# One transfer for the gate and up weights of a pair of experts, by halves of the contraction

## The reference, cut to what matters

```python
for e in range(N_EXPERTS):                       # 32
    gu = xt @ w_gate_up[e]                       # (n, 1024) @ (1024, 512)
    h = jax.nn.silu(gu[:, :D_EXPERT]) * gu[:, D_EXPERT:]   # D_EXPERT = 256
    y = y + gate[:, e:e + 1] * (h @ w_down[e])   # (n, 256) @ (256, 1024)
```

## Time and profile before

| | us |
|---|---|
| median of 3 runs | 611.1 (610.58 to 611.39) |
| the profiled execution, its own time | 611.46 |
| span of that execution in the trace | 609.8 |
| TensorE busy (share of the span) | 528.2 (87%) |
| VectorE busy | 363.7 (60%) |

### The profile page before, as it was taken

The page is one execution under the profiler, slowest core; times in us unless marked ns, Lnnn a source line. Parts: engine busy times, 40 slices in busy tenths (PEclk is TensorE's granted clock), DMA queues, the critical chain, the costliest instruction groups (busy, mean ns, idle before and its releaser), DMA issues.

```text
span 609.8 us, 8917 instructions
## 1 busy us (share of the span) xinstructions
PE 528.2 (87%) x3276; PEld 288.7 (47%) x3276; DVE 363.7 (60%) x718; ACT 187.9 (31%) x351; POOL 135.1 (22%) x156
## 2 busy tenths in 40 slices
PE   5999999999969988899999989989998667768772
PEld 4887888884335543345545843333332122222210
DVE  1641028388963466654247857577877676665686
ACT  1100075204143553114121232245444333332340
POOL 1001046140013761000000200333333221222231
PEclk9999999999979997999999989999999999999997
DMA  8940007670333923100787699999999999999951
GB/s 309 396 161 5 0 1 281 210 311 0 146 133 118 419 94 135 52 2 35 298 355 278 240 397 413 417 344 405 415 416 413 416 421 416 416 414 419 411 218 49
DMA packets 34010, 158.21 MB, mean 259 GB/s; under 512 B 12680, under 2 KB 12680, under 8 KB 20016
## 3 DMA queue, kind: packets, MB, share of 16 engines
q1 hardware_dynamic: 20592, 127.72, 52.3%
q0 software_dynamic: 10752, 29.59, 13.0%
q10 hardware_dynamic: 2624, 0.34, 0.4%
HBM read 160.38 MB, written 21.23 MB: 298 GB/s over the span
## 4 chain that ended last, share of the span: by engine, by line
PE 62%; DMA 21%; DVE 8%; ACT 5%; issue 3%; SPq 0%; POOL 0%; DVEq 0%; ACTq 0%; POOLq 0%
PE ps L488 22%; DMA arena_o<-in_w_gu 19%; PE ps L940 11%; PE ps L726 8%; PE ps L963 5%; PE ps L567 2%; PE ps L613 2%; PE ps L629 2%; DVE arena_s L1436 2%; ACT arena_s L1208 2%; PE ps L925 1%; PE ps L533 1%; DMA x_rows<-arena_s 1%; PE ps L650 1%; PE ps L789 1%
## 5 line engine op out<-in xcount | busy, mean ns | idle before, releaser
L940 PE MATMUL ps<-arena_w,arena_s 128*64 128x512 f32 x368 | 109.2, 605 | 24.6 <-DMA arena_w<-in_w_gu 11.5
L488 PE MATMUL ps<-arena_w 128*128 128x260 f32 (+1 forms) x448 | 100.4, 387 | 6.3 <-DMA arena_w<-in_w_in 6.3
L488 PEld LDWEIGHTS ps<-arena_w 128*128 128x128 f32 (+1 forms) x448 | 84.3, 189 | 21.9 <-DMA arena_w<-in_w_in 6.3
L940 PEld LDWEIGHTS ps<-arena_w,arena_s 128*64 128x64 f32 x368 | 33.3, 139 | 97.5 <-issue 67.7
L963 PE MATMUL ps<-arena_w,cs 128*64 128x512 f32 x184 | 56.5, 619 | 20.8 <-ACT cs L1224 20.8
L726 PE MATMUL ps<-arena_o,arena_s 128*128 128x512 f32 x128 | 59.6, 612 | 1.6 <-DVE arena_s L1560 1.6
L940 PE MATMUL ps<-arena_o,arena_s 128*64 128x512 f32 x112 | 50.2, 596 | 0.0
L1436 DVE STREAM_TRANSPOSE arena_s<-arena_w 128x1024 f32<-128x1024 f32 x36 | 41.9, 1216 | 10.7 <-PE ps L567 10.7
L2110 POOL DMA_INDIRECT first_rows<-arena_s,known x15 | 17.8, 1189 | 112.3 <-ACT arena_s L1231 103.6
L1869 DVE TENSOR_TENSOR arena_s<-arena_s,ps 128x256 f32<-128x256 f32 x16 | 6.7, 421 | 58.4 <-ACT arena_s L1220 55.2
L963 PEld LDWEIGHTS ps<-arena_w,cs 128*64 128x64 f32 x184 | 16.2, 140 | 51.1 <-issue 30.4
(11 more groups left out here) (340 smaller groups left out, 885.5 us busy)
## 6 DMA issues: line engine op xcount, KB each, us to landing
arena_w<-in_w_gu SPq DMA_DIRECT2D x46, 1024.0 KB
arena_w<-in_w_dn SPq DMA_DIRECT2D x23, 1024.0 KB
arena_o<-in_w_gu SPq DMA_DIRECT2D x14, 1024.0 KB
arena_o<-in_w_dn SPq DMA_DIRECT2D x7, 1024.0 KB
arena_w<-in_w_in SPq DMA_DIRECT2D x13, 512.0 KB, 15.1
arena_o<-in_w_out SPq DMA_DIRECT2D x1, 4096.0 KB, 13.6
arena_s<-in_w_gu SPq DMA_DIRECT2D x4, 1024.0 KB, 7.5
arena_w<-in_xT SPq DMA_DIRECT2D x4, 520.0 KB, 6.5
```

The costliest lines, as they stand in the source:

```text
L488: last = mm(ps[rows, b + n, 0:HALF], lhs(k), rhs(k)[:, n * HALF:(n + 1) * HALF], start=(k == 0), stop=(k == ks - 1))
L940: last = mm(ps[64 * e:64 * e + 64, 2 + q, :], xgT[:, k, CAP * e:CAP * (e + 1)], gu_w[2 * slots + e][:, k, :], start=(k == 0), stop=(k == K ...
```

## The change

The six slots stay. A slot's 16 KB of gate and up weights now hold one half of the contraction for both experts of a pair, and the table `GU_SLOT` says which slot has which half. A half of a pair is one transfer of 128 partitions with 16 KB each, 2 MB; the weights lie in memory in that order, so each is one contiguous stretch. Down weights stay as they were, one transfer of 1 MB for each expert, in the slot of that expert. The waits of SyncE stand where they stood; TensorE waits for 16 in place of 32 for a half. In the first loads, slot 2 gets the first half of the second pair (before: both halves of its first expert), slot 5 the first half of the third, slot 3 and slot 4 the second halves.

```diff
+GU_SLOT = [[0, 1], [2, 3], [5, 4]]
...
-        gu_w = [s[:, 0:KD * 2 * DE].rearrange("p (k n) -> p k n", k=KD) for s in slot]
+        gu_w = [s.rearrange("p (e k n) -> p e k n", e=2, k=KD // 2) for s in gu_flat]
...
-            def gate_up(j, e, half):
-                cols = slice(half * KD * DE, (half + 1) * KD * DE)
-                sp.dma_start(gu_flat[j][:, cols], w_gu[e].rearrange("o p n -> p (o n)")[:, cols]).then_inc(gu_landed[half][j // 2], 16)
+            def gate_up(q, half, pr):
+                sp.dma_start(gu_flat[GU_SLOT[q][half]], w_gu[half, pr].rearrange("o p n -> p (o n)")).then_inc(gu_landed[half][q], 16)
...
             for half in range(2):
-                for j in (0, 1):
-                    gate_up(j, slice(j, j + 1), half)
+                gate_up(0, half, slice(0, 1))
             for j in (0, 1):
                 down(j, slice(j, j + 1))
-            for half in range(2):
-                gate_up(2, slice(2, 3), half)
+            gate_up(1, 0, slice(1, 2))
             down(2, slice(2, 3))
             store_x1(1)
             store_x1(2)
             sp.wait_ge(dec_mixed, 1)
-            for half in range(2):
-                gate_up(5, slice(5, 6), half)
+            gate_up(2, 0, slice(2, 3))
             down(5, slice(5, 6))
             store_x1(3)
             sp.wait_ge(o_done, 16)
-            for half in range(2):
-                gate_up(3, slice(3, 4), half)
+            gate_up(1, 1, slice(1, 2))
             down(3, slice(3, 4))
...
-            def refill(q, e, used):
+            def refill(q, pr, used):
                 for half, done in enumerate((gu_half, gu_ps)):
                     sp.wait_ge(done, used)
-                    for n in range(2):
-                        gate_up(2 * q + n, slice(e + n, e + n + 1) if isinstance(e, int) else bass.ds(e + n, 1), half)
+                    gate_up(q, half, slice(pr, pr + 1) if isinstance(pr, int) else bass.ds(pr, 1))
                 sp.wait_ge(dn_ps, used)
...
                     for e in range(2):
                         last = mm(ps[64 * e:64 * e + 64, 2 + q, :], xgT[:, k, CAP * e:CAP * (e + 1)],
-                                  gu_w[2 * slots + e][:, k, :], start=(k == 0), stop=(k == KD - 1))
+                                  gu_w[GU_SLOT[slots][k // (KD // 2)]][:, e, k % (KD // 2), :], start=(k == 0), stop=(k == KD - 1))
...
-        "w_gu": i["w_gate_up"][pairs].reshape(NE, KD, P, 2 * DE).transpose(0, 2, 1, 3).reshape(NE, P, -1),
+        "w_gu": i["w_gate_up"][pairs].reshape(NE // 2, 2, 2, KD // 2, P, 2 * DE).transpose(2, 0, 4, 1, 3, 5).reshape(2, NE // 2, P, -1),
```

More of the change, by code:

```diff
@@ L252, in hymba_step @@
             [arena_s[:, S_SLOT + W_SLOT * n:S_SLOT + W_SLOT * (n + 1)] for n in range(2)]
-        gu_w = [s[:, 0:KD * 2 * DE].rearrange("p (k n) -> p k n", k=KD) for s in slot]
-        dn_w = [s[:, KD * 2 * DE:W_SLOT].rearrange("p (k n) -> p k n", k=2) for s in slot]
         gu_flat, dn_flat = [s[:, 0:KD * 2 * DE] for s in slot], [s[:, KD * 2 * DE:W_SLOT] for s in slot]
+        gu_w = [s.rearrange("p (e k n) -> p e k n", e=2, k=KD // 2) for s in gu_flat]
+        dn_w = [s.rearrange("p (k n) -> p k n", k=2) for s in dn_flat]
         xg = [part(arena_s, s, D) for s in S_XG]
@@ L437, in _ @@
             landed(sp, gathered[0])
-            for half in range(2):
-                gate_up(4, slice(4, 5), half)
+            gate_up(2, 1, slice(2, 3))
             down(4, slice(4, 5))
@@ L442, in _ @@
             sp.dma_start(lng2, lns[2:4].partition_broadcast(P)).then_inc(ln1_landed, 16)
-            def refill(q, e, used):
+            def refill(q, pr, used):
                 for half, done in enumerate((gu_half, gu_ps)):
                     sp.wait_ge(done, used)
-                    for n in range(2):
-                        gate_up(2 * q + n, slice(e + n, e + n + 1) if isinstance(e, int) else bass.ds(e + n, 1), half)
+                    gate_up(q, half, slice(pr, pr + 1) if isinstance(pr, int) else bass.ds(pr, 1))
                 sp.wait_ge(dn_ps, used)
                 for n in range(2):
-                    down(2 * q + n, slice(e + n, e + n + 1) if isinstance(e, int) else bass.ds(e + n, 1))
-            refill(0, 6, 1)
-            refill(1, 8, 2)
+                    down(2 * q + n, slice(2 * pr + n, 2 * pr + n + 1) if isinstance(pr, int) else bass.ds(pr * 2 + n, 1))
+            refill(0, 3, 1)
+            refill(1, 4, 2)
             sp.wait_ge(routed, 1)
@@ L457, in _ @@
             with sp.Fori(0, n_rounds * (NE // 4) - 3) as it:
-                refill(0, (it * 4 + 10) % NE, it * 2 + 4)
-                refill(1, (it * 4 + 12) % NE, it * 2 + 5)
-            refill(0, NE - 2, past + (NPAIR - 2))
+                refill(0, (it * 2 + 5) % NPAIR, it * 2 + 4)
+                refill(1, (it * 2 + 6) % NPAIR, it * 2 + 5)
+            refill(0, NPAIR - 1, past + (NPAIR - 2))
             landed(sp, outs_stored, 6)
@@ L931, in products @@
                 q, slots = n % 2, n if n < HEAD else (n - HEAD) % 2
-                landed_count = 32 if n < HEAD else nth(it, n - HEAD, 2, 32, 64) if not isinstance(it, tuple) else \
-                    it[0] * 16 + ((n - HEAD) // 2 * 32 + 64)
+                halves_landed = 16 if n < HEAD else nth(it, n - HEAD, 2, 16, 32)
+                downs_landed = 32 if n < HEAD else nth(it, n - HEAD, 2, 32, 64)
                 pe.wait_ge(xt_sb, nth(it, n, add=1))
@@ L937, in products @@
                     if k % (KD // 2) == 0:
-                        pe.wait_ge(gu_landed[k // (KD // 2)][slots], landed_count)
+                        pe.wait_ge(gu_landed[k // (KD // 2)][slots], halves_landed)
                     for e in range(2):
                         last = mm(ps[64 * e:64 * e + 64, 2 + q, :], xgT[:, k, CAP * e:CAP * (e + 1)],
-                                  gu_w[2 * slots + e][:, k, :], start=(k == 0), stop=(k == KD - 1))
+                                  gu_w[GU_SLOT[slots][k // (KD // 2)]][:, e, k % (KD // 2), :], start=(k == 0), stop=(k == KD - 1))
                     if k == KD // 2 - 1:
@@ L947, in products, with experts @@
                     turn_tokens(it, n + 1)
-                return slots, landed_count
-            def experts(it, n, slots, landed_count):
+                return slots, downs_landed
+            def experts(it, n, slots, downs_landed):
                 pe.wait_ge(h_ready, nth(it, n, add=1))
@@ L956, in experts @@
                 pe.wait_ge(ht_sb, nth(it, n, add=1))
-                pe.wait_ge(dn_landed[slots], landed_count)
+                pe.wait_ge(dn_landed[slots], downs_landed)
                 if n > 0:
```

## The result

The changed kernel takes 617.25 us (median of 4 runs, 615.59 to 618.85) against 610.84 of the kernel before in the same runs: a ratio of 1.0105, with an interval of 1.0089 to 1.0121. The forecast was 609.7 with a range of 607.8 to 612.8. In the profiled execution the span is 616.2 us, 6.4 us above the 609.8 of before.

A forecast was written before the change was run, and what follows sets the result against it. Weight loads on saturated DMA until 570.38 us, then a fixed tail, were taken as the bound. Packets 1.37 plus the store 0.05 save 1.4 us: 611.1 median to 609.7, range 607.8 to 612.8.

The forecast's parts named there:

- What bounds the kernel, and the tail behind 570.38: Gate and up weight loads saturate DMA from 399.72 to the landing at 570.38 us; behind it a fixed 39.4 us tail.
- Packets: Weight queue, 399.72 to 570.38: 16 KB rows stay one packet, 9.5 ns saved each, 1.37 us over 18 transfers.
- Tokens: Token transfers beside the weight queue, 400 to 570 us: 6.72 MB beside 63.25 MB, bytes and packets unchanged; no time priced.
- Waits: SyncE's waits for weight slots stand where they stood, none added; half the issues go, behind a backlog: nothing gained.
- small transfers wait longer, 615.1: Around GpSimd's table store, reload and first scatter: pieces let 16 KB packets by, fifth pair's tokens 5.4 us late; chance 0.13.
- The rule of taking turns: DMA engines alternate between queues by packets of several descriptors, a weak form of the small-transfers rival; time stays 609.7.
- The fixed 2.0 us for a transfer: Skill page's fixed cost per DMA; taken off for 18 saved transfers, 36 us gain, time 575; the prediction rejected it.
- Clock: TensorE's last down matmuls, granted clock 0.53 from 592.8 to 596.4: longer costs up to 1.7 us, shorter gains nothing.

## Why the prediction was wrong, step by step

*What bounds the kernel, and the tail behind 570.38:* right for the kernel before. With 8 KB rows and with fewer token packets the end hangs on the weights. The step was wrong in taking this bound as the only one near. The token queue stood at 0.71 of its turns, and nothing in my text looked at how far it was from full.

*Packets:* right. The cut to 128 packets came, and 431 and 420 GB/s. At 431 GB/s a packet of 16 KB takes 608.2 ns on its engine, 10.0 less than two of 8 KB at 424 (618.3), and the run with 4 KB rows gave 12, against the 9.5 of the forecast. The gain of 0.6 us in the pair of runs with fewer tokens is below the 1.37 forecast, but their intervals don't tell the two apart.

*Tokens, "neither their bytes nor their packets change":* this is the step that failed. It was true and priced at nothing; but what a token transfer gets is turns, and their number is set by the other queue (5977 packets beside 5822). By halving the packets of gate and up I took away 18 of the 54 turns a pair that GpSimd's queue had beside weights (16 packets and 2 completion writes), and left 36 for its 36. What I had put at nothing turned the gain of 1.4 us into a loss of 6.4 (617.25 against 610.84).

*Waits, "no wait is added":* true of the text of the kernel. The waits for landed scatters that stood there (GpSimd before each scatter, ScalarE before each reload) began to hold. They are where the loss shows, but not its cause, since it stayed with these waits relaxed.

*The rival "small transfers wait longer, 615.1":* its mechanism is the one that came, its place was wrong. Around the table GpSimd waits 5.82 and 7.88 us in place of 5.62 and 8.03, and 6.90 in place of 4.39 for the first scatter; TensorE's turn of the fifth pair's tokens stands at 403.32 against 402.82. The loss came in the saturated part, the very place that I had given as having "spare time". I had set the chance at 0.13 because the wait for the table's store is less than 32 pieces at 0.31 us each. In fact tiny pieces can come out as fewer packets (the runs that tried to fill the queue show it), so that row was weak evidence against taking turns.

*The rule of taking turns* in the page "DMA: Bandwidth & Descriptors" of the Trainium skill, section "Queues, rings and completion order", was in the text with the result left at 609.7. The counts of 5822 to 5977 bear out equal turns; whether a turn is one packet as the profile counts them, or a group of several, no run here shows.

*The fixed 2.0 us for a transfer:* the section "Anatomy of one DMA" of the page "DMA: Bandwidth & Descriptors" of the Trainium skill states it for transfers issued by GpSimd. The 424 GB/s were those of loads issued by SyncE, so they rule out the time of 575 here and don't test the page's figure.

*Clock:* 0.91 in the window, a follower of TensorE's waits: after 10.2 us of idling until 548.38 its down matmuls take 1.06 us each, and from 552.85 on 0.59. The chain of the changed kernel has no TensorE piece between 428.66 and 584.35, so the clock doesn't set the delay there. Behind it a lower clock (granted 0.57 from 598.3 to 604.7 us, before 0.68 from 592.8 to 598.2) accounts for about 1.0 us (6.39 against 5.35).

## What to carry to other kernels

Before making the packets of a bulk load larger, count packets by queue in the saturated window, not only bytes: here the queue of small transfers, once it was backed up, passed about one packet for each packet of the bulk load (5977 beside 5822). If its own need is near that number, the larger packets can cost more than they save (here 6 us for a gain near 1), and relaxing the waits on the small transfers didn't help, since the queue itself was full. Places out of bounds count as packets too in an indirect transfer that has others in bounds.

## What the hardware showed beyond that

Loads of 16 KB rows into 64 partitions at a time, two for each half, ran at half the rate, with all DMA time taken. The window of that kernel, whose profiled execution took 835.5 us:

```profile
400.00:570.00 170.00, 98.28 (x382) 34.99 (x382) 64.77 (x97) 35.96 (x61) 24.60 (x22) 0.75 1.02 231
```

231 GB/s at a share of 1.02, where the 128-partition loads have 416. No run looked into why. And a gather with no place in bounds had 2 packets an engine, while the token transfers, each with some places in bounds, had 8.8 of 9.
